# The 64-row sample tile of the output and down projections, computed as two column halves on two partition halves

## What is computed

```python
# u: gated sum of the two mixer branches, (rows, 1024)
x = x + rmsnorm(u @ w_out, g_post_mix)                 # output projection, w_out 1024 x 1024
h = rmsnorm(x, g_pre_ffn)
z = causal_conv3(h @ w_up)                             # w_up 1024 x 5632
x = x + rmsnorm(swiglu(z) @ w_down, g_post_ffn)        # down projection, w_down 2816 x 1024
```

## Time and profile before

| | us |
|---|---|
| median of 3 runs | 2156.53 (2155.9 to 2161.16) |
| span of the profiled execution | 2214.7 |
| PE busy / PEld busy in it | 1978.6 (89%) / 1347.8 |
| ACT busy / DVE busy / POOL busy | 590.4 / 896.0 / 406.6 |
| output projection, from its first product to the up projection's first | 1544.3 to 1631.9 |
| down projection, from its first product on | 1991.8 to 2196.7 |
| from there to the last DVE instruction's end | to 2211.4 |

### The profile page before, as it was taken

How to read it: one execution, slowest core, us unless ns; L and a number is a source line. 1 busy time by engine, 2 the same in 40 slices (tenths; PEclk the granted TensorE clock), 3 DMA queues, 4 the chain that set the end, 5 groups by cost and what they waited for, 6 DMA issues and landing times.

```text
span 2214.7 us, 25971 instructions
## 1 busy us (share of the span) xinstructions
PE 1978.6 (89%) x9819; PEld 1347.8 (61%) x9819; DVE 896.0 (40%) x1602; ACT 590.4 (27%) x1251; POOL 406.6 (18%) x514
## 2 busy tenths in 40 slices
PE   5888888986979899998688889899979999999996
PEld 4666667765867655555355556676457777773332
DVE  4888888775000233354354445111223434330002
ACT  2222222221110233454344445200531111110103
POOL 2333222331000210112555553000000000000000
PEclk8988889887989655699899999999989999999998
DMA  5665555553440100000466776712032222220211
GB/s 180 227 210 183 191 197 179 179 208 107 150 121 4 39 1 1 1 1 27 154 208 208 226 227 186 222 60 92 24 95 62 72 57 77 57 76 29 76 36 43
DMA packets 201015, 248.82 MB, mean 112 GB/s; under 512 B 32202, under 2 KB 173851, under 8 KB 192539
## 3 DMA queue, kind: packets, MB, share of 16 engines
q1 hardware_dynamic: 176684, 134.16, 20.6%
q0 software_dynamic: 21248, 109.46, 14.5%
q10 hardware_dynamic: 2960, 3.54, 0.4%
HBM read 236.09 MB, written 19.29 MB: 115 GB/s over the span
## 4 chain that ended last, share of the span: by engine, by line
PE 60%; issue 18%; DVE 15%; ACT 3%; POOL 1%; another core or an unknown queue 1%; DMA 1%; SPq 1%; ACTq 1%; POOLq 0%; DVEq 0%
PE ps L1509 12%; PE ps L1956 9%; DVE mem L1100 8%; PE ps L1743 6%; PE ps L1520 5%; PE ps L1830 4%; PE ps L1901 3%; PE ps L1852 3%; PE ps L1541 3%; PE ps L1726 2%; PE ps L1755 2%; PE ps L1807 2%; DVE mem L1104 2%; ACT mem L924 1%; PE ps L1591 1%
## 5 line engine op out<-in xcount | busy, mean ns | idle before, releaser
L1509 PE MATMUL ps<-mem 128*128 128x288 f32 x1536 | 401.8, 425 | 10.7 <-DVE mem L1123 9.1
L1509 PEld LDWEIGHTS ps<-mem 128*128 128x128 f32 x1536 | 306.0, 200 | 99.4 <-issue 9.4
L1931 PE MATMUL ps<-mem 128*128 128x288 f32 x1408 | 349.5, 409 | 0.0
L1931 PEld LDWEIGHTS ps<-mem 128*128 128x128 f32 x1408 | 267.1, 191 | 73.0
L672 POOL DMA_INDIRECT mem<-in_cache_sel_kv,sidx x192 | 185.3, 965 | 343.3 <-PE ps L1690 192.8
L1100 DVE TENSOR_REDUCE mem<-mem 128x512 f32<-128x2048 f32 x64 | 235.8, 3684 | 1.4
L1956 PE MATMUL ps<-mem 128*128 128x512 f32 (+1 forms) x440 | 205.1, 611 | 0.0
L1956 PEld LDWEIGHTS ps<-mem 128*128 128x128 f32 (+1 forms) x440 | 72.5, 180 | 132.0 <-issue 131.9
L635 POOL DMA_INDIRECT mem<-in_cache_cmp_kv,pidx x64 | 79.5, 1241 | 343.8 <-DVE mem L1100 336.6
L1743 PE MATMUL ps<-mem 64*128 64x128 f32 (+3 forms) x256 | 139.0, 636 | 2.1 <-DVE nmx L1259 2.1
L1852 PE MATMUL ps<-mem 128*64 128x512 f32 x288 | 83.1, 652 | 60.1 <-ACT mem L924 37.8
(11 more groups left out here) (299 smaller groups left out, 2408.7 us busy)
## 6 DMA issues: line engine op xcount, KB each, us to landing
mem<-in_cache_sel_kv SPq DMA_DIRECT2D x320, 128.0 KB
mem<-in_w_up SPq DMA_DIRECT2D x44, 512.0 KB, 5.1
mem<-in_w_in SPq DMA_DIRECT2D x32, 512.0 KB, 5.6
mem<-in_w_in SPq DMA_DIRECT2D x14, 1024.0 KB, 6.0
mem<-in_w_down SPq DMA_DIRECT2D x10, 1024.0 KB, 5.0
mem<-in_state_win_kv SPq DMA_DIRECT2D x16, 512.0 KB
out<-in_state_win_kv POOLq DMA_DIRECT2D x8, 1008.0 KB, 16.0
mem<-in_x_prompt SPq DMA_DIRECT2D x8, 512.0 KB, 6.5
```

What stands on the lines that cost most here:

```text
L1509: mm = t.matmul(ps[:, 2 * (u % 2) + a, 0:NHF], lhs(k), hT[:, k, a * NHF:(a + 1) * NHF], start=(k == 0), stop=(k == KD - 1))
L1931: mm = t.matmul(ps[:, 2 * (u % 2) + a, 0:NHF], lhs(k), hT[:, k, a * NHF:(a + 1) * NHF], start=(k == 0), stop=(k == KD - 1))
```

## The change

Only the 64-row tile is computed otherwise, and the order within a down-projection block is turned round:

- Output projection, tile 4: 16 products as before, but columns 0 to 511 go to partitions 0 to 63 and columns 512 to 1023 to partitions 64 to 127 of the same bank, and the order is k outside, half `s` inside, so the two halves alternate.
- Down projection: in each weight block the order is tile outside, k inside. Tile 4's product of 512 columns becomes two of 256 columns, on partitions 0 to 63 and 64 to 127.
- ACT brings the two partition halves together: for tile 4 of the output projection two copies of 64x512 into `wos`, a wait on `wos_ok`, and then the Square reads `wos`. In the down projection two copies of 64x256 into `fo` (half 0) or `fo1` (half 1), a wait on `fo1_ok`, and one Square from there. DVE's L1413 and, for half 1, L1461 read these copies in place of PSUM.

```diff
@@ ACT, output projection @@
-                link(a.activation(junk2[0:n].rearrange("p (a c) -> p a c", a=2), ps[0:n, 2 * w:2 * w + 2, :], ACT.Square,
-                                  accum_out=st_ss[0:n, 1, i:i + 1]))
+                if i < PT:
+                    ...
+                else:
+                    for s in range(2):
+                        ins = a.activation(wos[0:S, 512 * s:512 * s + 512], ps[64 * s:64 * s + 64, 2 * w, :], ACT.Copy)
+                    ins.then_inc(wos_ok, 1)
+                    act.wait_ge(wos_ok, 1)
+                    link(a.activation(junk2[0:S], wos[0:S], ACT.Square, accum_out=st_ss[0:S, 1, i:i + 1]))
...
@@ ACT, down projection @@
-                    if h == 0:
+                    if i == PT:
+                        to = fo[0:S, i, :] if h == 0 else fo1[0:S, :]
+                        for s in range(2):
+                            ins = a.activation(to[:, 256 * s:256 * s + 256], ps[64 * s:64 * s + 64, bank, 0:256], ACT.Copy)
+                        ins.then_inc(fo1_ok, 1)
+                        act.wait_ge(fo1_ok, h + 1)
+                        a.activation(junk3[0:S, 0:512], to, ACT.Square, accum_out=st_ss[0:S, 3 * h, i:i + 1]).then_inc(fo_ok, 1)
+                    elif h == 0:
...
@@ PE, output projection @@
+                if i == PT:
+                    for k in range(KD):
+                        ws = wslot[(B_WO + k // 2) % NSLOT].rearrange("p (k c) -> p k c", c=D)
+                        for s in range(2):
+                            mm = t.matmul(ps[64 * s:64 * s + 64, 2 * w, :], ohg[:, k, T:N], ws[:, k % 2, s * 512:(s + 1) * 512],
+                                          start=(k == 0), stop=(k == KD - 1))
+                    mm.then_inc(wo_ok, 1)
+                    continue
...
@@ PE, down projection @@
-                    steps = [(k, i) for k in range(k0, k0 + nk) for i in range(TT)]
-                    if h == 1 and q == len(DN_T) - 1:
-                        steps.sort(key=lambda x: x[1])
-                    for k, i in steps:
...
+                    for i in range(TT):
                         bank = (TT * h + i) % 8
-                        if k == 0 and TT * h + i >= 8:
+                        if k0 == 0 and TT * h + i >= 8:
                             pe.wait_ge(fo_ok, TT * h + i - 8 + 1)
+                        for k in range(k0, k0 + nk):
+                            if h == 0 and i == 0:
+                                pe.wait_ge(g_ok, k + 1)
+                            if i < PT:
+                                mm = t.matmul(ps[:, bank, :], gT[:, k, i * P:(i + 1) * P], ws[:, k - k0, :],
+                                              start=(k == 0), stop=(k == NF - 1))
+                                continue
+                            for s in range(2):
+                                mm = t.matmul(ps[64 * s:64 * s + 64, bank, 0:256], gT[:, k, T:N],
+                                              ws[:, k - k0, s * 256:(s + 1) * 256], start=(k == 0), stop=(k == NF - 1))
```

More of the change, by code:

```diff
@@ L243, in build @@
         junk2 = view(D)
+        wos = view(D)
         at[0] = a_f
@@ L259, in build @@
         ftmp = view(512)
+        fo1 = view(512)
         ps = ctx.enter_context(nc.psum_tensor("ps", [P, 8, 512], F32))
@@ L279, in build @@
         up_ok = sem("up_ok")
+        wos_ok = sem("wos_ok")
+        fo1_ok = sem("fo1_ok")
         ssum_ok = sem("ssum_ok")
@@ L956, in _ @@
                 act.wait_ge(wo_ok, i + 1)
-                link(a.activation(junk2[0:n].rearrange("p (a c) -> p a c", a=2), ps[0:n, 2 * w:2 * w + 2, :], ACT.Square,
-                                  accum_out=st_ss[0:n, 1, i:i + 1]))
+                if i < PT:
+                    link(a.activation(junk2[0:n].rearrange("p (a c) -> p a c", a=2), ps[0:n, 2 * w:2 * w + 2, :], ACT.Square,
+                                      accum_out=st_ss[0:n, 1, i:i + 1]))
+                else:
[4 more added lines that the diff above has]
+                    link(a.activation(junk2[0:S], wos[0:S], ACT.Square, accum_out=st_ss[0:S, 1, i:i + 1]))
                 factor(n, st_ss[0:n, 1, i:i + 1], st_rs[0:n, 1, i:i + 1])
@@ L1005, in _ @@
                         a.activation(junk3[0:n, 0:512], ps[0:n, bank, :], ACT.Square, accum_out=st_ss[0:n, 3, i:i + 1]).then_inc(fo_ok, 1)
+                    if h == 1:
                         act.wait_ge(ssum_ok, i + 1)
@@ L1412, in _ @@
                     hv = hn[i % 2][0:n]
-                    link(v.scalar_tensor_tensor(hv.rearrange("p (a c) -> p a c", a=2), ps[0:n, 2 * w:2 * w + 2, :],
+                    got = ps[0:n, 2 * w:2 * w + 2, :] if i < PT else wos[0:S].rearrange("p (a c) -> p a c", a=2)
+                    link(v.scalar_tensor_tensor(hv.rearrange("p (a c) -> p a c", a=2), got,
                                                 st_rs[0:n, 1, i:i + 1], gqm[0:n].rearrange("p (a c) -> p a c", a=2), ALU.mult, ALU.mult))
@@ L1459, in _ @@
                 for h in range(2):
-                    src = fo[0:n, i, :] if h == 0 else ps[0:n, (TT + i) % 8, :]
+                    src = fo[0:n, i, :] if h == 0 else ps[0:n, (TT + i) % 8, :] if i < PT else fo1[0:S, :]
                     link(v.scalar_tensor_tensor(ftmp[0:n, :], src, st_rs[0:n, 3, i:i + 1], gqf[0:n, h * 512:(h + 1) * 512], ALU.mult, ALU.mult))
@@ L1945, in _ @@
                     ws = wslot[b % NSLOT].rearrange("p (k c) -> p k c", c=512)
-                    steps = [(k, i) for k in range(k0, k0 + nk) for i in range(TT)]
-                    if h == 1 and q == len(DN_T) - 1:
-                        steps.sort(key=lambda x: x[1])
-                    for k, i in steps:
-                        if h == 0 and i == 0:
-                            pe.wait_ge(g_ok, k + 1)
-                        n = TR[i]
+                    for i in range(TT):
                         bank = (TT * h + i) % 8
-                        if k == 0 and TT * h + i >= 8:
+                        if k0 == 0 and TT * h + i >= 8:
                             pe.wait_ge(fo_ok, TT * h + i - 8 + 1)
-                        mm = t.matmul(ps[0:n, bank, :], gT[:, k, i * P:i * P + n], ws[:, k - k0, :], start=(k == 0), stop=(k == NF - 1))
-                        if k == NF - 1:
+                        for k in range(k0, k0 + nk):
[8 more added lines that the diff above has]
+                                              ws[:, k - k0, s * 256:(s + 1) * 256], start=(k == 0), stop=(k == NF - 1))
+                        if q == len(DN_T) - 1:
                             mm.then_inc(dn_ok, 1)
```

## The result

| | before | after |
|---|---|---|
| median, us | 2156.22 (4 runs) | 2126.16 (4 runs, 2122.97 to 2133.72) |
| ratio | | 0.9857, 95% interval 0.9835 to 0.9879 |
| span of the profiled execution | 2214.7 | 2131.9 |
| output projection, wo 4's first product to the up projection's first | 28.20 | 25.72 |
| down projection, first product to half 1's first Square | 198.12 | 168.14 |

The spans themselves are 83 us apart.

What follows compares the result with a forecast made beforehand. PE was taken to bound the down projection until half 1's tile 0 ends, then ACT; in the output projection PE until wo 4. Gains 28.5 + 2.4 - 0.8 = 30.1 us gave 2156.5 - 30.1 = 2126.4, range 2119 to 2139.

Steps and rivals of the forecast that it cites:

- The watched point: Down projection: the end of tile 0 in the last block, not PE's last product, sets the time; ACT bounds afterwards.
- Concurrency: Sample-tile products on the two partition halves run side by side, 0.216 us per 256-column pair; 17.9 us of the down-projection gain.
- The pair priced from L1852 taken whole: Down projection, lower bound of the gain: a 256-column pair costs 0.25 us, making the gain 2.9 us less.
- Batching: Down projection: sample visits grouped by weight block save 31 changes of shape at 0.342 us each, 10.6 us.
- Down projection: Sample-tile work ahead of the end of half 1's tile 0 falls from 50.4 to 21.9 us, gain 28.5 us.
- the allowance of 1.5 for the clock: Part of the forecast's own range: 1.5 us either way, named where the up projection's first 8 us run at clock 0.73.
- Output projection: wo 4: PE saves 6.9 us, ACT busy with tile 3 allows 3.6, copies cost 1.2; gain 2.4 us.
- The end: Half 1's tile 4: two 64x256 ACT copies on the critical chain cost 0.8 us.
- The rule against it: Skill page: weight loads overlap matmuls in flight only when row groups differ; the column halves here share their rows.
- The two rivals that rest on serial records or bare loads: Halves not concurrent: 8.6 us gain, 2147.9, chance 0.06. Weight loads unhidden at 0.14 us: gain 18.3, 2138.2, chance 0.08.
- The third, a price for each change of partition half: Each switch of partition half costs 0.171 us and halves are not concurrent: 8.5 us slower, 2165.0, chance 0.03.
- The step from the profile to the median: Median lies 58 us below the profiled span; the same 30.1 us is taken off it, as profiling stretches nothing touched.

Runs made afterwards that it cites:

- the second series: The unmodified changed kernel run once more beside the kernel before: median 2124.72 us in ten runs, 32.0 us below 2156.77.
- the run on the same partition half: Against the kernel before: down projection batched, each sample product cut into two of 256 columns, both on partitions 0 to 63; median 2147.48 us, ratio 0.9939.

## Why the prediction was right

It gave 2126.4, and 2126.16 was measured. The three terms came as forecast where the clocks are alike (28.4 + 2.5 - 0.8 = 30.1). That the whole time fits to 0.2 us is luck: the second series has 32.0 for the same change. Point by point:

- *The watched point.* The time hung on the end of half 1's tile 0, not on PE's last product. Leaving the last batch out changed nothing.
- *Concurrency.* A pair of 256 columns was taken at 0.216. With 4 k, 15.80 a block was forecast and 15.80 came. The pair priced from L1852 taken whole, 0.25, was the wrong reading: it counted the change of shape a second time for every pair.
- *Batching.* 10.6 us forecast, 10.4 measured alone; the price of a change of shape, 0.342, came back as 0.34 and 0.35 by two other edits.
- *Down projection.* 28.5 us forecast. 198.12 - 168.14 = 30.0 in the first two profiles and 198.28 - 169.84 = 28.4 in the second two. The difference is PE's clock over the first records: the first 32 took 13.79 us in the one profile and 15.49 in the other. The granted clock there was 1.00 in the one and 0.88 in the other, about as in the kernel before (0.89). It is chance, and about the size of the allowance of 1.5 for the clock; the forecast's 28.5 is met by the 28.4.
- *Output projection.* 6.9 us of PE work saved, 3.6 to be had, 1.2 paid for copies: 2.4 forecast, 2.48 measured. With the table loads away ACT no longer withheld the rest.
- *The end.* 0.8 forecast, 0.83 and 0.85 measured.
- *The rule against it.* That weight loads overlap only across row groups, from the Trainium skill's page "TensorE: Matmul & The Clock Gate", section "Part 3: Packing small matmuls — row/col tiling", does not hold here: sixteen loads of the same rows passed in 1.49 us beside 1.87 us of streaming. The estimate from that section's 2.38 for three column tiles would have made the pair 0.27; it is 0.216, what one record alone takes. The two rivals that rest on serial records or bare loads fall with the run on the same partition half, since it has every cost but the overlap. The third, a price for each change of partition half, has no room: a batch's eight pairs of records take 1.88 us, and 8 x 0.216 is 1.73.
- *What was off.* "The profiled execution would go from 2214.7 to 2184.6" was not so: it went to 2131.9. The step from the profile to the median held for another reason than given. I had only said that the touched stretches are not stretched by profiling; the 58 us were two longer attention stretches of that one execution, and two profiles of the same program would have shown it. Also wrong was a forecast made later, that one half after the other costs either everything or nothing: PE overlapped four records.

## What to carry to other kernels

A row tile of 64 rows streams as many columns as one of 128; cut its columns in two, put the halves on the two partition halves in turn, and the streaming costs half, but only if the two alternate closely (here within two products, four records) and if the engine that reads the result has time to put it together. Keep such tiles together: each visit from 128-row work and back cost 0.34 us here, as much as 400 columns of one record. Before counting a PE saving in full, find who waits for it: here 6.9 us of PE work was worth 3.6 until the reader's table loads were gone.

## What the runs showed of the hardware that was not expected

PE overlapped the two halves only where their records were at most four apart in the program's order, the same four for records of 0.216 us and of 0.429 us. And a stretch of 2192 matrix records with page gathers beside it took 276 to 283 us in ten profiles and 323 to 331 in four, at 234 to 240 and at 201 to 205 GB/s, for identical instructions; three of the four long ones came from one series on one chip. That series' whole times point at something that lasts longer than one execution: all eleven of the kernel before stood some 40 to 50 us higher than executions at like clock on another chip (2164.28 to 2173.41 at 0.919 to 0.926 beside one of 2122.73 at 0.923, 2201.12 at 0.908 beside 2150.45 to 2163.02 at 0.904 to 0.913). What sets it stays open: no run tells whether it is the place of the cached pages in memory, the chip, or the order in which two DMA queues meet. The mean granted clock is a second source of spread: 0.92 in place of 0.90 to 0.91 went with some 30 us less for one and the same kernel. Until it is known, a change of some 10 us in this kernel is better read from its own stretch than from the whole time.
